# Seven places for expert weights instead of six in a hybrid convolution and expert layer, with the residual stream kept in memory meanwhile

## What is computed

```python
def _hier_moe(h, w_coarse, b_coarse, w_fine, b_fine, w_gate, w_up, w_down):
    ...
    grp = jnp.argmax(coarse_logits, axis=-1)
    ...
    top_v, top_i = lax.top_k(fine_sel, TOP_K_FINE)
    p_exp = jax.nn.softmax(top_v, axis=-1) * p_grp
    ...
    for e in range(N_EXPERTS):
        hid = jax.nn.silu(t @ w_gate[e]) * (t @ w_up[e])
        out = out + combine[:, e:e + 1] * (hid @ w_down[e]).astype(jnp.float32)

# the layer, on x:
    x = x + jnp.concatenate([z_a, z_b], axis=-1) @ w_out
    x = x + _hier_moe(_rmsnorm(x, g_ffn), w_coarse, b_coarse, w_fine, b_fine, w_gate, w_up, w_down)
# and at the end
y_prompt = _rmsnorm(xp, g_final)
y_sample = _rmsnorm(xs, g_final)
```

## Time and profile before

| | us |
|---|---|
| three runs, median | 564.33 (563.63 to 565.37) |
| profiled execution | 564.4 |
| its span | 562.6 |
| TensorE busy | 492.2 |
| VectorE, ScalarE, GpSimd busy | 246.5, 100.5, 190.1 |
| DMA moved | 141.17 MB, mean 251 GB/s |

### The profile page before, as it was taken

The page is one execution under the profiler, slowest core; times in us unless marked ns, Lnnn a source line. Parts: engine busy times, 40 slices in busy tenths (PEclk is TensorE's granted clock), DMA queues, the critical chain, the costliest instruction groups (busy, mean ns, idle before and its releaser), DMA issues.

```text
span 562.6 us, 9132 instructions
## 1 busy us (share of the span) xinstructions
PE 492.2 (87%) x3423; PEld 294.9 (52%) x3424; DVE 246.5 (44%) x496; ACT 100.5 (18%) x204; POOL 190.1 (34%) x283
## 2 busy tenths in 40 slices
PE   6999999999999999996689889897869687488992
PEld 3787777777776455553344444443434343244430
DVE  4139999999955112347222222222112212022237
ACT  5131111011125332334011101111001101011123
POOL 2013818837678001112233233332313313033101
PEclk9999999999999999997799999999979989599997
DMA  8993016000002991139588999999999999998077
GB/s 330 320 398 73 0 32 268 2 0 1 1 1 96 371 406 42 40 131 399 175 337 276 371 367 408 395 394 392 385 388 395 382 398 387 399 402 333 31 277 235
DMA packets 35504, 141.17 MB, mean 251 GB/s; under 512 B 10322, under 2 KB 10338, under 8 KB 23193
## 3 DMA queue, kind: packets, MB, share of 16 engines
q1 hardware_dynamic: 29194, 127.91, 60.1%
q0 software_dynamic: 4960, 9.45, 5.1%
q10 hardware_dynamic: 1327, 3.49, 1.6%
HBM read 134.47 MB, written 13.17 MB: 262 GB/s over the span
## 4 chain that ended last, share of the span: by engine, by line
PE 66%; DMA 17%; issue 6%; SPq 4%; DVE 4%; ACT 2%; POOL 1%; POOLq 0%; DVEq 0%; ACTq 0%
PE bank L1222 25%; DMA region_w<-in_w_up 11%; PE bank L1305 9%; PE bank L1418 8%; PE bank L1438 7%; PE bank L1413 7%; DMA region_w<-in_w_in 3%; SPq L388 3%; DMA slot<-y_rows 2%; PE bank L1215 2%; PE bank L1404 2%; PE bank L1366 1%; PE bank L1331 1%; PE bank L1428 1%; DVE ua L1107 1%
## 5 line engine op out<-in xcount | busy, mean ns | idle before, releaser
L1222 PE MATMUL bank<-region_h,region_w 128*128 128x256 f32 (+1 forms) x576 | 140.6, 406 | 0.0
L1222 PEld LDWEIGHTS bank<-region_h,region_w 128*128 128x128 f32 x576 | 109.2, 190 | 29.8
L1107 DVE TENSOR_TENSOR ua<-ua,bank 128x128 f32<-128x128 f32 x30 | 8.7, 289 | 184.1 <-ACT ua L619 184.1
L1418 PE MATMUL bank<-region_w,z 128*32 128x256 f32 x512 | 48.7, 431 | 14.8 <-DMA region_w<-in_w_up 11.3
L1305 PE MATMUL bank<-region_w,z 128*128 128x512 f32 x128 | 56.7, 596 | 0.2 <-ACT z L564 0.2
L1438 PE MATMUL bank<-region_w,ua 128*32 128x512 f32 x344 | 51.9, 598 | 0.0
L770 POOL COPY gcol<-gidx 64x1 uint32 (+1 forms) x30 | 5.4, 179 | 137.4 <-DVE sb_rows L1098 137.4
L905 DVE SCALAR_TENSOR_TENSOR z<-ub,par,z 128x512 f32<-128x512 f32 x60 | 47.5, 792 | 0.0
L905 DVE SCALAR_TENSOR_TENSOR region_x<-ub,par,region_x 128x512 f32<-128x512 f32 x56 | 46.6, 832 | 0.0
L701 POOL TENSOR_TENSOR ub<-region_x 128x512 f32<-128x512 f32 x4 | 25.3, 6335 | 58.5 <-ACT ub L518 31.9
L1305 PEld LDWEIGHTS bank<-region_w,z 128*128 128x128 f32 x128 | 23.8, 190 | 28.0 <-issue 26.3
(11 more groups left out here) (230 smaller groups left out, 655.5 us busy)
## 6 DMA issues: line engine op xcount, KB each, us to landing
region_w<-in_w_down SPq DMA_DIRECT2D x21, 1024.0 KB, 17.4
region_w<-in_w_gate SPq DMA_DIRECT2D x16, 1024.0 KB, 14.9
region_w<-in_w_up SPq DMA_DIRECT2D x16, 1024.0 KB, 17.2
region_w<-in_w_in SPq DMA_DIRECT2D x4, 2048.0 KB, 19.0
slot<-in_w_gate SPq DMA_DIRECT2D x6, 1024.0 KB, 14.9
slot<-in_w_up SPq DMA_DIRECT2D x6, 1024.0 KB, 14.6
slot<-in_w_down SPq DMA_DIRECT2D x6, 1024.0 KB, 15.8
region_x<-in_w_up SPq DMA_DIRECT2D x5, 1024.0 KB, 24.7
```

The costliest lines, as they stand in the source:

```text
L1222: ins = mm(ps[2 * bank + j][:, 0:LEN[j]], sec[name][:, k, c * P:(c + 1) * P], hT[:, k, CUT[j]], start=(k == 0), stop=(k == KC - 1))
L1418: ins = mm(ps[1][r0:r0 + H, 0:2 * P].rearrange("p (w f) -> p w f", w=2), xT[:, k, half * H:(half + 1) * H], wgu[i][:, :, k, h, :], start=( ...
```

## The change

- `NSLOT` is 7. The seventh place is in `region_h`, where x1 lies, and a part of `ub`; its down weights are loaded as two halves. Expert e goes to place e mod 7.
- x1 is stored to memory (`x1_rows`) by SyncE as its tiles are done: four stores ahead of expert 3's loads, the fifth behind them. The gate of place 5 waits for both gathers instead of one, and behind it, once the five stores have landed, stand the four loads of expert 6.
- After the loads of expert 31 SyncE waits until the blocks up to expert 27, the last in the seventh place, are done, and loads x1 back into `region_h`; VectorE and TensorE wait for that before the final stage.
- TensorE's pairs: the first stands alone, with its three register loads ahead of the first tokens; then a loop of seven pairs run twice; then one pair. The waits for gate and up of the second expert stand behind the first expert's own blocks, as before.
- y is asked for in the order (tile, part) 0.0, 0.1, 2.0, 1.0, 2.1, 1.1, 4.0, 4.1, 3.0, 3.1, and the tiles are finished in the order 0, 2, 1, 4, 3. ScalarE's and VectorE's counts follow that order.

```diff
-NSLOT = 6
+NSLOT = 7
+FINISH = (0, 2, 1, 4, 3)
...
-        slot_gu = [reg[:, lo:lo + 2 * PART] for reg, lo, _, _ in places]
+        LAST = NSLOT - 1
+        slot_gu = [reg[:, lo:lo + 2 * PART] for reg, lo, _, _ in places] + [RH[:, 0:2 * PART]]
         slot_dn = [reg[:, lo:lo + PART] for _, _, reg, lo in places]
+        last_dn = [RH[:, 2 * PART:2 * PART + D], ub_t[:, 0:D]]
...
+            def store_x1(t):
+                sp.wait_ge(s_x1, 2 * t + 2)
+                sp.dma_start(x1_dram[t * P:t * P + TROWS[t], :], x1[0:TROWS[t], t, :]).then_inc(s_x1d, 16)
+
+            for t in range(NT - 1):
+                store_x1(t)
             sp.wait_ge(s_o, NT)
             load_expert(3, 3)
+            store_x1(NT - 1)
...
-            sp.wait_ge(s_gath[0], 16)
+            for i in range(2):
+                sp.wait_ge(s_gath[i], 16)
             load_part(5, 0, 5)
+            sp.wait_ge(s_x1d, 16 * NT)
+            load_expert(LAST, LAST)
             sp.wait_ge(s_tab, 1)
...
+            used = sp.value_load(bound[0:1, NE // NSLOT * NSLOT:NE // NSLOT * NSLOT + 1], min_val=1, max_val=NBLK)
+            sp.wait_ge(s_down, used)
+            for t in range(NT):
+                sp.dma_start(x1[0:TROWS[t], t, :], x1_dram[t * P:t * P + TROWS[t], :]).then_inc(s_x1r, 16)
...
-            for t in range(NT):
-                for k in range(2):
-                    sp.dma_start(yg[k][t][0:TROWS[t], :], y_dram[k * NTOK + t * P:k * NTOK + t * P + TROWS[t], :])\
-                      .then_inc(s_yg[k][t], 16)
-
-            for t in range(NT):
+
+            for t, k in ((0, 0), (0, 1), (2, 0), (1, 0), (2, 1), (1, 1), (4, 0), (4, 1), (3, 0), (3, 1)):
+                sp.dma_start(yg[k][t][0:TROWS[t], :], y_dram[k * NTOK + t * P:k * NTOK + t * P + TROWS[t], :])\
+                  .then_inc(s_yg[k][t], 16)
+
+            for t in FINISH:
...
             dve.wait_ge(s_gfin, 16)
+            dve.wait_ge(s_x1r, 16 * NT)
...
             pe.wait_ge(s_tab, 1)
+            first_pair = blocks_of(0)
             pe.wait_ge(s_mv, 1)
...
-            with pe.Fori(0, NE // NSLOT) as it:
-                for i in range(0, NSLOT, 2):
-                    pair(it, i)
-            for i in range(0, NE % NSLOT, 2):
-                pair(NE // NSLOT, i)
-
-
+            pair(0, (0, 1), (0, 0), first_pair)
+
+            with pe.Fori(0, 2) as it:
+                for e in range(2, 2 + 2 * NSLOT, 2):
+                    pair(it * (2 * NSLOT) + e, (e % NSLOT, (e + 1) % NSLOT),
+                         (it * 2 + e // NSLOT, it * 2 + (e + 1) // NSLOT))
+            pair(NE - 2, ((NE - 2) % NSLOT, (NE - 1) % NSLOT), (NE // NSLOT, NE // NSLOT))
+
+
+            pe.wait_ge(s_x1r, 16 * NT)
```

More of the change, by code:

```diff
@@ L385, in load_part @@
             def load_part(i, part, e):
+                src = parts[part][:, bass.ds(e, 1), :].rearrange("p e n -> p (e n)")
+                if (i, part) == (LAST, 2):
+                    for c, dst in enumerate(last_dn):
+                        sp.dma_start(dst, src[:, c * D:(c + 1) * D]).then_inc(s_wexp[i][part], 16)
+                    return
                 dst = slot_dn[i] if part == 2 else slot_gu[i][:, part * PART:(part + 1) * PART]
-                sp.dma_start(dst, parts[part][:, bass.ds(e, 1), :].rearrange("p e n -> p (e n)"))\
-                  .then_inc(s_wexp[i][part], 16)
+                sp.dma_start(dst, src).then_inc(s_wexp[i][part], 16)
             def load_expert(i, e):
@@ L634, in _ @@
             nc.scalar.activation(small[:, 62:63], eps_rms, ACT.Sqrt)
-            for t in range(NT):
+            for at, t in enumerate(FINISH):
                 n = TROWS[t]
@@ L651, in _ @@
                     continue
-                act.wait_ge(s_fin, t - sum(p < t for p in BY_PE) + 1)
+                act.wait_ge(s_fin, t // 2 + 1)
                 nc.scalar.activation(yg[0][t][0:n, :], x1[0:n, t, :], ACT.Square,
                                      accum_out=small[0:n, 16 + t:17 + t]).then_inc(s_sq3, 1)
-                rms(16, n, t, s_sq3, s_rms3)
+                act.wait_ge(s_sq3, at + 1)
+                nc.scalar.activation(small[0:n, 40 + t:41 + t], small[0:n, 16 + t:17 + t], ACT.Sqrt,
+                                     scale=1.0 / D, bias=eps_rms[0:n, :]).then_inc(s_rms3, 1)
         @block.gpsimd
@@ L1161, in _ @@
             add_row(2, 1)
-            normed(1)
             add_row(4, 0)
@@ L1165, in _ @@
             add_row(4, 1)
-            normed(3)
-            normed(4)
+            for t in (1, 4, 3):
+                normed(t)
         @block.tensor
@@ L1399, in _, with down_rows @@
             wdn = [w.rearrange("p (c d) -> p c d", c=F // P) for w in slot_dn]
+            def down_rows(i, c, h):
+                if i == LAST:
+                    return last_dn[c][:, h * 512:(h + 1) * 512]
+                return wdn[i][:, c, h * 512:(h + 1) * 512]
             H = T // 2
@@ L1405, in tokens, with block_of @@
                 return ins
-            def block_of(g, halves, turn):
+            def block_of(g, halves, turns):
                 pe.wait_ge(s_xt, g + 1)
@@ L1432, in block_of @@
                 pe.wait_ge(s_yc, g + 1)
-                for i in sorted(set(halves)):
-                    pe.wait_ge(s_wexp[i][2], turn * 16 + 16)
+                for half in range(1 if halves[0] == halves[1] else 2):
+                    i, turn = halves[half], turns[half]
+                    pe.wait_ge(s_wexp[i][2], turn * 32 + 32 if i == LAST else turn * 16 + 16)
                 for c in range(F // P):
@@ L1438, in block_of, with blocks_of @@
                         ins = mm(ps[3][quarter * H:(quarter + 1) * H, :], hidT[:, c * T + r0:c * T + r0 + H],
-                                 wdn[halves[quarter % 2]][:, c, h * 512:(h + 1) * 512],
+                                 down_rows(halves[quarter % 2], c, h),
                                  start=(c == 0), stop=(c == F // P - 1))
                 ins.then_inc(s_down, 1)
+            def blocks_of(e):
+                return (pe.value_load(bound[0:1, bass.ds(e, 1)], min_val=0, max_val=NBLK - 1),
+                        pe.value_load(bound[0:1, bass.ds(e + 1, 1)], min_val=1, max_val=NBLK),
+                        pe.value_load(bound[0:1, bass.ds(e + 2, 1)], min_val=1, max_val=NBLK))
@@ L1443, in _, with pair @@
             keep_busy(24)
             pe.wait_ge(s_tab, 1)
+            first_pair = blocks_of(0)
             pe.wait_ge(s_mv, 1)
             tokens(0, KC).then_inc(s_xt_ps, 1)
-            def pair(it, i):
-                e = it * NSLOT + i
-                first = pe.value_load(bound[0:1, bass.ds(e, 1)], min_val=0, max_val=NBLK - 1)
-                after = pe.value_load(bound[0:1, bass.ds(e + 1, 1)], min_val=1, max_val=NBLK)
-                end = pe.value_load(bound[0:1, bass.ds(e + 2, 1)], min_val=1, max_val=NBLK)
+            def pair(e, slots, turns, ends=None):
+                first, after, end = ends or blocks_of(e)
+                i, j = slots
@@ L1454, in pair @@
                 for part in range(2):
[L1455 removed]
+                    pe.wait_ge(s_wexp[i][part], turns[0] * 16 + 16)
                 with pe.If(after > first + 1):
                     with pe.Fori(first, after - 1) as g:
[L1458 removed]
+                        block_of(g, (i, i), (turns[0], turns[0]))
                 for part in range(2):
[L1460 to L1461 removed]
+                    pe.wait_ge(s_wexp[j][part], turns[1] * 16 + 16)
```

16 lines of the change are left out of this document (8 added, 8 removed).

## The result

| | before | changed |
|---|---|---|
| median of five runs each, us | 563.63 (562.65 to 565.37) | 573.78 (573.52 to 578.46) |
| profiled execution, us | 564.4 | 578.5 |
| its span, us | 562.6 | 576.7 |

The ratio is 1.0196, with a 95% interval of 1.0165 to 1.0227: the change makes the kernel 10 us slower, where 554.7 us had been forecast. The profiled execution of the changed kernel is its slowest, 4.7 us over its median; where that matters it is said.

The account below looks back on a forecast made before the run. The prediction took the expert weight stream at 390 GB/s as the bound, with TensorE waiting for expert 27's up part; 564.4 - 9.7 + 0 = 554.7 us, all other terms taken as 0 or within the 9.7, range 551.0 to 559.5.

Parts of the forecast that it names:

- Seventh place: In the weight stream: expert 6 no longer waits for block 0, filling the hole from 274 to 306 us; gain 9.7 us.
- Register loads ahead of the first tokens: Before TensorE's first block: loads moved ahead of the token wait; gain 1.2 to 1.9 us, counted inside the 9.7.
- x1 to memory: Five stores on SyncE's queue, four of them while DMA is quiet; cost 0, up to 0.7 us.
- x1 back: Five loads behind expert 31's, from about 511 to 517 us, before y is asked for at 527.8; cost 0.
- both gathers: Start of the seventh place's loads: waiting for the second gather too costs 0 to 1.5 us, taken as 0.
- The final stage: From the last y landing to the end: new order of loads and tiles, -0.3 to +1.3 us, taken as 0.
- The code: TensorE's longer loop of pairs: instruction fetch taken as 0, upper bound 1.5 us a pair, hidden ahead of expert 27's landing.
- Does it reach the end?: At experts 26 and 27 TensorE still waits 8 us for expert 27's up part, so the end moves by 9.7 us.
- Rival 1: Instruction fetch on the path in the last three pairs: mild form 1.5 us each, 4.5 us, 559.2 us; chance 0.09.
- its slower form: Same three pairs, each waiting for a packet in a full queue: over 3.2 us a pair, 566.7 at 4; chance 0.05.

Follow-up runs that it names:

- e5: Changed kernel with the seventh place used only for experts 6 and 13, seven pairs laid out, then a loop of three; 560.04 us, ratio 0.9909.
- e9: The kernel of e5 with the final stage in the old order; 561.2 us, ratio 0.9953.
- e6: Changed kernel with all 16 TensorE pairs laid out one after the other, no loop; 565.36 us, ratio 1.0012.
- e2: Changed kernel with the seventh place used once, for expert 6, and a short loop of three pairs; 563.56 us, ratio 0.9968.
- e4: Kernel before with only the new order of the final stage; 563.3 us, ratio 0.9972.
- e3: Changed kernel with the old order of the final stage; 575.6 us, ratio 1.0189.
- e1: Kernel before, six places, with only TensorE's loop lengthened to six pairs run twice and four pairs behind; 572.85 us, ratio 1.0125.
- e8: Kernel before with weight loads from expert 6 on cut to a quarter of their columns; 544.0 us (one run).
- e7: Changed kernel with weight loads from expert 7 on cut to a quarter of their columns; 567.9 us (one run).

## Why the prediction was wrong, step by step

*Seventh place.* Right in the changed kernel. The queue was full from 272 us on, place 2 was reloaded at 303.0 us (302.5 forecast), and expert 27's up part landed at 475.3 (476.4 forecast). The term of 9.7 us measured 10.8, of which 2.3 are the earlier first block. Counted from the first block, the landing came 8.5 us earlier (201.6 us instead of 210.1). Where TensorE waited for it again, it was less: 204.2 us in e5, 206.1 in e9 and 206.4 in e6, so 3.7 to 5.9 us. Even without the cost of the code, then, the 9.7 us would not have reached the end in these versions, and why the stream's lead shrinks wasn't tried. e2 adds what the sum hadn't said: the gain lasts as long as the place stays in rotation.

*Register loads ahead of the first tokens.* Right: 2.63 us of idle time before the first block became 0.88.

*x1 to memory, x1 back, both gathers.* Right, cost 0: the gate of place 5 and expert 6 were issued at 271.12 and 271.49 us, x1's loads at 511.79, and DMA was quiet again at 520, 27 us ahead of the first y.

*The final stage.* Taken at 0, between -0.3 and +1.3. e4 gained 1.6 us (interval 0.0 to 0.6%, 0.1 to 3.2 us), which overlaps the range, though its middle lies outside. The sum had four matmuls behind the last landing; in e4 and in the changed kernel the chain has eight.

*The code.* This is the step that failed. It was taken at 0 with an upper bound of 1.5 us a pair, read from the entry of the loop before the first block. The one jump back of the long loop was seen, but it was given no price. It measures 11.79 us in the changed kernel, 11.89 in e3, 9.45 with light weights and 7.55 in e1; a kernel whose loop stays has no row that could have sized it. The Trainium skill ("Runtime: NRT & Kernel Launch", section "Instruction fetch mechanics") says that a taken branch whose target is not in the current window of two pages forces a fetch of the page before execution goes on; the prediction quoted it for a target outside the instruction memory. That there is a stall at the far jump agrees with the traces. The two pages do not: the loop of before, six packets of 16 KB long, jumps back with no packet fetched. The traces agree with the 128 KiB that the same section of the Trainium skill gives for TensorE's instruction memory: six packets, 0.10 MB, stay, and the loops of six and seven pairs, two packets a pair, do not.

Two further terms were missing altogether. One is a late entry into pairs that follow on short ones: experts 18 and 19, behind three pairs of one block each, at 4.55 us, and experts 26 and 27, two pairs behind another of them, at 4.89 us, instead of 1.2. A pair brings about two packets of code whether its blocks run or are skipped. Between 300 and 500 us in the changed kernel, away from the back edge, q8 has them about 6 us or more apart, 8 in the 60 us from 400 on, where a pair of one block lasts about 8.5. That fits the run of short pairs ahead of the gaps before experts 16 and 18 in e1, e5 and e6. It does not say why experts 24 and 25 are entered at 1.20 us right behind a pair of one block, and at the back edge two packets came only some 3 us apart. No run changed the size of a block's code, so this is argued and not shown. The other is the clock: after each such gap the next products run slow, 5.85 us instead of the 3.83 that 64 of them take in e6 at 518.56 us, at a granted clock of 0.63 instead of 1.00.

*Does it reach the end?* It fell with the step before. TensorE was to be at experts 26 and 27 at 468.5 us, 8 us before the weights, and that slack was counted as a cover for everything that the code could cost. It came at 489.7. Before, from the first block to there took 198.9 us, 8.0 of them waits for weights. Now it took 216.1 with no such wait. The cover of 8 us was used up by the back edge alone, and the rest went straight to the end. Rival 1 had the mechanism; its slower form, more than 3.2 us a pair over three pairs and 566.7 us, was given 0.05. It had the price at each pair of the last three, where it is one large price at one place, ahead of expert 27, plus 3.4 to 3.7 us at two others.

The rows could not have given the price, but they show how far they reach. 0.10 MB of code came for the three pairs of the old loop, and from then on none: that is a statement about a size that fits. A loop of twice the length is outside it, and the cheapest neighbour inside the trace was no upper bound for it.

## What to carry to other kernels

A loop whose body a trace shows to be fetched once is a resource: before lengthening it, count its packets of code (here 6 for three pairs were kept, the 12 or more of six and seven pairs were not) and price the jump back at 8 to 12 us a pass (7.55, 9.45, 11.79 and 11.89 here), with the slow matmuls behind it. Keep the rotation of buffers and the length of the loop apart: laying out the part that needs the odd rotation and looping over the rest gave the faster kernel here, 560.0 us against 563.6 for the kernel before (564.7 on that chip) and 573.8 for the change. And slack in front of a wait covers one surprise only, so give it a size on both sides before charging every unknown to it.

## What the runs showed of the hardware

- A jump back in a loop too long to stay costs TensorE 7.5 to 11.9 us, and 9.45 us with the DMA engines 0.68 busy over the gap and idle at its end. In a loop that stays it is 1.75 to 1.87 us, register loads included, and 1.1 to 1.3 at the other pairs (before, e8). The packets are 16 KB (0.64 MB in 39) and take about 1 us each; in the last 4 us of the gap of 9.45 only one moved. The time is between the packets, not in them.
- Code fetched in order behind TensorE (e6) is hidden for most of the 254.6 us. It shows behind runs of pairs that pass in one block, by 3.8 and 4.4 us. That the fetching is what is late there is argued, not shown.
- A loop of six packets fetches nothing after its first pass, one of about 12 or more fetches in every pass. Where between them the limit lies wasn't tried.
- Behind idle gaps of 2.81 us (e2), 3.76 (e6), 5.18 (e1), 9.45 (e7) and 11.79 (changed), the 64 products of the next block take 5.43, 5.38, 5.30, 6.42 and 5.85 us, at a granted clock of 0.69, 0.69, 0.70, 0.57 and 0.63. At 1.00 they take 3.83 (e6, 518.56 us).
